# First output tiles multiplied inside the last head pair: an attention layer and its projection in one program

## The reference

```python
z = u_lat @ w_in                                             # 8 x 1024 columns
y_a = z_ab * dwconv(z_ac * z_ax, w_conv) * silu(z_ag)        # short gated convolution
y_b = neighbourhood_attention(q, k, v, k_c, v_c, rpb) * silu(z_bg)   # 16 heads, 8 x 16 window + context
y_lat = concat([y_a, y_b]) @ w_out                           # 2048 x 1024
h_lat = h_lat + gate * y_lat                                 # then RMSNorm and modulation of layer 1
```

## Time and profile before

| | us |
|---|---|
| median of three runs | 2330.8 |
| lowest and highest | 2329.86, 2332.24 |
| profiled execution, its own time | 2330.06 |
| its span | 2328.3 |
| last `weigh` of the attention begins | 1252.63 |
| first product of the projection | 1264.40 |

### The profile page before, as it was taken

One profiled execution on the slowest core, in us unless ns is written; L12 is line 12 of the kernel. 1 busy time (PEld: TensorE's weight loads), 2 busy tenths in 40 slices (PEclk: granted clock), 3 DMA queues, 4 the chain that ended last, 5 costly groups with the idle time before them and its releaser, 6 DMA issues. The chain is left out here.

```text
span 2328.3 us, 33600 instructions
## 1 busy us (share of the span) xinstructions
PE 2248.5 (97%) x11996; PEld 1958.6 (84%) x11996; DVE 1511.3 (65%) x2407; ACT 1167.5 (50%) x1711; POOL 484.9 (21%) x287
## 2 busy tenths in 40 slices
PE   6999999999999999999997999799999999999998
PEld 4788888888888888888885888699999999998787
DVE  4576575765757657577577437648667766776755
ACT  4534544345344453444434324347876777678311
POOL 0232231322313223223230300021122112220000
PEclk9999999999999999999998999899999999999999
DMA  7111221112122112122115656201111111113521
GB/s 292 37 55 52 66 62 65 54 52 66 50 69 63 52 57 58 34 80 64 62 28 205 181 152 180 88 28 55 54 55 55 55 46 64 55 55 127 208 82 63
DMA packets 145223, 187.47 MB, mean 81 GB/s; under 512 B 50360, under 2 KB 108856, under 8 KB 142008
## 3 DMA queue, kind: packets, MB, share of 16 engines
q1 hardware_dynamic: 137592, 166.67, 22.3%
q10 hardware_dynamic: 7488, 18.88, 2.2%
HBM read 155.62 MB, written 29.88 MB: 80 GB/s over the span
## 5 line engine op out<-in xcount | busy, mean ns | idle before, releaser
L956 PE MATMUL ps<-u_hi,w_hi 128*128 128x512 f32 (+1 forms) x1464 | 533.7, 365 | 0.0
L956 PE MATMUL ps<-u_hi,w_lo 128*128 128x512 f32 (+1 forms) x1464 | 519.1, 355 | 0.0
L956 PE MATMUL ps<-u_lo,w_hi 128*128 128x512 f32 (+1 forms) x1464 | 517.8, 354 | 0.0
L956 PEld LDWEIGHTS ps<-u_hi,w_lo 128*128 128x128 f32 x1464 | 276.2, 189 | 40.1
L956 PEld LDWEIGHTS ps<-u_lo,w_hi 128*128 128x128 f32 x1464 | 277.0, 189 | 35.0
L956 PEld LDWEIGHTS ps<-u_hi,w_hi 128*128 128x128 f32 x1464 | 276.5, 189 | 35.1
L2163 PE MATMUL ps<-u_hi,o_w_hi 128*128 128x426 f32 (+2 forms) x640 | 238.2, 372 | 9.4 <-POOL o_w_lo L1738 9.4
L571 ACT ACTIVATE probs<-probs,neg_max 128x640 f32<-128x640 f32 (+1 forms) x160 | 122.8, 768 | 245.4 <-DVE neg_max L772 245.4
L2163 PE MATMUL ps<-u_hi,o_w_lo 128*128 128x426 f32 (+2 forms) x640 | 237.8, 372 | 0.0
L2163 PE MATMUL ps<-u_lo,o_w_hi 128*128 128x426 f32 (+2 forms) x640 | 237.7, 371 | 0.0
L1738 POOL TENSOR_TENSOR o_w_lo<-o_w_raw,o_w_hi 128x1024 fp32r<-128x1024 f32 x48 | 134.5, 2801 | 476.1 <-ACT o_w_hi L1757 476.1
(11 more groups left out here) (221 smaller groups left out, 4601.7 us busy)
## 6 DMA issues: line engine op xcount, KB each, us to landing
w_stage<-in_w_even SPq DMA_DIRECT2D x63, 512.0 KB, 3.5
o_w_raw<-in_w_odd SPq DMA_DIRECT2D x48, 512.0 KB, 3.5
ada_piece<-in_w_ada SPq DMA_DIRECT2D x20, 1024.0 KB, 5.4
y_tile<-y_scratch SPq DMA_DIRECT2D x40, 512.0 KB, 5.2
wout_raw<-in_w_out SPq DMA_DIRECT2D x8, 1024.0 KB, 10.1
y_scratch<-h_backward SPq DMA_DIRECT2D x16, 512.0 KB, 2.6
final_w_raw<-in_w_out SPq DMA_DIRECT2D x8, 1024.0 KB, 10.7
final_y_raw<-y_scratch SPq DMA_DIRECT2D x15, 512.0 KB, 4.3
```

What stands on the lines that cost most here:

```text
L956: last = nc.tensor.matmul(ps[:, bank(j, g), 0:t - f], w[:, slot, c * P:(c + 1) * P], x[:, c, f:t], start=(c == 0 and n == 0), stop=(c == K ...
```

## The change

The blocks `even_layer` and `out_projection(layer=0)` become one. The function `out_projection` is gone; its parts are now in `even_layer`.

- The last pair's 12 conv units all lie in steps 0 to 7 (`LAST_UNITS`). POOL splits the weights of CB and CG two steps earlier (`SPLIT_AFTER_LAST`).
- Steps 8 to 19 of PE multiply the first 56 chunks of pass 0 (`OUT_CHUNKS`: tile, first and last chunk): tiles 0, 1 and 2 and half of tile 3. The rest follows in `projection()`, first tile 3's other half.
- W of pass 0 is loaded over u's latent columns, in two portions as CG's groups 0 and 1 finish with them, and y's even tiles over u's context columns; odd tiles lie over the weights of the layer.
- ACT and DVE split W and y inside the steps: `within(s)` before the units or `copy_low`/`output`, `behind(s)` after them. Two of the gate-row matmuls and the read of tiles 0 and 1 out of their banks lie in the steps too.
- Conv rows are stored in three portions, attention rows of pair 7 in three, so that y's tiles can be loaded earlier.
- W of pass 1 is now loaded once all attention rows are stored, behind the load of y tile 4.
- `odd_layer` has another memory map; its instructions and their order are unchanged.

The diff, cut to its core:

```diff
+LAST_UNITS = ((0,), (1,), (2, 3), (4,), (5, 6), (7,), (8, 9), (10, 11))
...
+OUT_CHUNKS = {8: (0, 0, 5), 9: (0, 5, 11), 10: (0, 11, YC), 11: (1, 0, 5), 12: (1, 5, 11), 13: (1, 11, YC),
+              14: (2, 0, 5), 15: (2, 5, 10), 16: (2, 10, 13), 17: (2, 13, YC), 18: (3, 0, 4), 19: (3, 4, 8)}
+OUT_BEGUN = 4
...
+    SPLIT_AFTER_LAST = {4: CB, 6: CG}
...
-        if not last:
-            return [(j, g, 0, KC) for j, g in (ORDER[s:s + 1] if s < STEPS - 1 else ORDER[s:])]
-        if s < 8:
-            return [(*ORDER[s], 0, KC)]
-        if s < LAT_STEPS:
-            return [(*ORDER[8 + (s - 8) // 2], s % 2 * (KC // 2), (s % 2 + 1) * (KC // 2))]
-        return []
+        if last:
+            return [(*ORDER[u], 0, KC) for u in LAST_UNITS[s]] if s < len(LAST_UNITS) else []
...
+            def projection():
+                i = PAIRS - 1
+                sp.wait_ge(proj, unit(i, CG, 0) + 1)
+                load_out_w(0, 0)
+                load_out_w(0, 1)
+                sp.wait_ge(w_lo, i * 8 + 8)
+                sp.wait_ge(ya_stored, 32 * i + 16)
+                load_y(0, 0, 0)
+                sp.wait_ge(proj, unit(i, CG, 1) + 1)
+                load_out_w(0, 2)
+                load_out_w(0, 3)
+                store_y(i, 0)
+                sp.wait_ge(yb_stored[0], 16 * PAIRS)
+                load_y(0, 0, 1)
+                sp.wait_ge(ya_stored, 32 * i + 48)
+                load_y(1, 1, 0)
+                load_y(1, 1, 1)
+                sp.wait_ge(a_mm, 2 * PAIRS)
+                load_x(0, 0, 0)
+                load_x(0, 1, 1)
+                for t in (2, 3):
+                    for half in range(2):
+                        load_y(t, t, half)
+                load_x(0, 2, 0)
+                store_rest(LAT // 2, LAT, LAT_STEPS)
+                load_x(0, 3, 1)
+                sp.wait_ge(yb_stored[1], 16 * i + 16)
+                for half in range(2):
+                    load_y(4, 4, half)
+                store_rest(LAT, TOK, STEPS)
+                for stored in yb_stored:
+                    sp.wait_ge(stored, 16 * PAIRS + (16 if stored is yb_stored[1] else 0))
+                for q in range(4):
+                    load_out_w(1, q)
+                load_x(0, 4, 0)
+                for t in range(5, NT):
+                    load_tile(0, t, t % 2)
...
+            def out_w_hi(p):
+                act.wait_ge(wo_loaded[p % 8 // 2], 32 * (p // 8 + 1))
+                if p < 8:
+                    nc.scalar.activation(w_pair(uhi, p), w_pair(w0raw, p), ACT.Copy).then_inc(wo_hi, 1)
+                else:
+                    c = slice(2 * p - 16, 2 * p - 14)
+                    nc.scalar.activation(w1hi[:, c, :], w1raw[:, c, :], ACT.Copy).then_inc(wo_hi, 1)
+            def out_y_hi(q, b, half):
+                if isinstance(q, int) and q < 2:
+                    act.wait_ge(proj, unit(PAIRS - 1, CG, NG - 1) + 1)
+                else:
+                    act.wait_ge(mm_done, q + 1)
+                act.wait_ge(y_loaded[half], q * 16 + 16)
+                nc.scalar.activation(y_half(0, b, half), raw_half(half), ACT.Copy).then_inc(y_hi, 1)
+            def copy_gate_row(s):
+                act.wait_ge(row_mm, s + 1)
+                nc.scalar.activation(grow[:, 0, s, :], ps[:, 7, :], ACT.Copy).then_inc(grow_done, 1)
+            def store_half(t):
+                act.wait_ge(h_done, t + 3)
+                act.dma_start(hs[t], h[:, t % 2, :]).then_inc(h_stored[t % 2], 16)
+            def within(s):
+                if s == 7:
+                    out_w_hi(0)
+                    out_w_hi(1)
+                elif s == 8:
+                    out_w_hi(3)
+                    out_y_hi(0, 0, 1)
+                elif s == 9:
+                    out_w_hi(5)
+                elif s == 10:
+                    out_w_hi(7)
+                elif s == 11:
+                    out_y_hi(1, 1, 1)
+                elif s == 13:
+                    out_y_hi(2, 0, 1)
+                elif s == 17:
+                    out_y_hi(3, 1, 1)
+            def behind(s):
+                i = PAIRS - 1
+                if s == 6:
+                    act.wait_ge(ya_done, i + 1)
+                    store_conv(act, i, 0, LAT // 2)
+                elif s == 7:
+                    out_y_hi(0, 0, 0)
+                    out_w_hi(2)
+                elif s == 8:
+                    out_w_hi(4)
+                    act.wait_ge(ya_done, i + 3)
+                    store_conv(act, i, LAT // 2, LAT)
+                    store_conv(act, i, LAT, TOK)
+                elif s == 9:
+                    out_w_hi(6)
+                elif s == 10:
+                    out_y_hi(1, 1, 0)
+                elif s == 12:
+                    copy_gate_row(0)
+                    out_y_hi(2, 0, 0)
+                elif s == 14:
+                    store_half(0)
+                elif s == 16:
+                    copy_gate_row(1)
+                    out_y_hi(3, 1, 0)
+                    store_half(1)
...
+                for t in range(2, NT):
+                    for half in range(2):
+                        out_y_hi(t + 2, t % 2, half)
+                    store_half(t)
+                    if 5 <= t < 9:
+                        out_w_hi(2 * t - 2)
+                        out_w_hi(2 * t - 1)
+                act.wait_ge(row_mm, 3)
+                nc.scalar.activation(grow[:, 1], ps[:, 6:8, :], ACT.Copy).then_inc(grow_done, 1)
...
+            def first_half(t, link):
+                b, s = t % 2, out_stream(t)
+                dve.wait_ge(xh_loaded[b], 16 * (t // 2) + 16)
+                dve.wait_ge(h_stored[b], 16 * (t // 2))
+                dve.wait_ge(grow_done, s + 1)
+                dve.wait_ge(mm_done, t + 3)
+                link(nc.vector.tensor_tensor(h[:, b, :], ps[:, b, :], grow[:, 0, s, :], ALU.mult))
+                nc.vector.tensor_tensor(h[:, b, :], h[:, b, :], xh[:, b, :], ALU.add).then_inc(h_done, 1)
+            half_link = Link(dve, out_links[0])
+            def within(s):
+                if s == 7:
+                    out_w_lo(0)
+                    out_w_lo(1)
+                elif s == 8:
+                    out_w_lo(3)
+                    out_y_lo(0, 0, 1)
+                elif s == 9:
+                    out_w_lo(5)
+                elif s == 10:
+                    out_w_lo(7)
+                elif s == 11:
+                    out_y_lo(1, 1, 1)
+                elif s == 13:
+                    out_y_lo(2, 0, 1)
+                    first_half(0, half_link)
+                elif s == 15:
+                    first_half(1, half_link)
+                elif s == 17:
+                    out_y_lo(3, 1, 1)
+            def behind(s):
+                if s == 7:
+                    out_y_lo(0, 0, 0)
+                    out_w_lo(2)
+                elif s == 8:
+                    out_w_lo(4)
+                elif s == 9:
+                    out_w_lo(6)
+                elif s == 10:
+                    out_y_lo(1, 1, 0)
+                elif s == 11:
+                    dve.wait_ge(ya_stored, 32 * PAIRS + 16)
+                    gate_diagonal(0, 0).then_inc(diag_done, 1)
+                elif s == 12:
+                    out_y_lo(2, 0, 0)
+                elif s == 14:
+                    gate_diagonal(0, 1).then_inc(diag_done, 1)
+                elif s == 16:
+                    out_y_lo(3, 1, 0)
...
+                    if last and s in OUT_CHUNKS:
+                        out_products(*OUT_CHUNKS[s])
...
+                    if last and s == 12:
+                        pe.wait_ge(row_done, PAIRS)
+                        gate_row(0)
+                    if last and s == 16:
+                        pe.wait_ge(mod_copied, PAIRS)
+                        gate_row(1)
                     if s == 14:
+                        if last:
+                            pe.wait_ge(grow_done, 1)
...
+            def out_products(t, c0, c1):
+                if c0 == 0 and t < 2:
+                    last_g = NG - 2 if t == 0 else NG - 1
+                    pe.wait_ge(bank_free[t], half(PAIRS - 1, CG, last_g) + 1)
+                elif c0 == 0:
+                    pe.wait_ge(h_done, t + 1)
+                for c in range(c0, c1):
+                    if c % 8 == 0:
+                        pe.wait_ge(y_lo, 2 * t + (c // 8 + 1))
+                    if t == 0 and c % 2 == 0:
+                        pe.wait_ge(wo_lo, c // 2 + 1)
+                    for n, (y, w) in enumerate(((0, 0), (0, 1), (1, 0))):
+                        ins = nc.tensor.matmul(ps[:, t % 2, :], y_chunk(y, t % 2, c), w_of(0, w, c),
+                                               start=(c == 0 and n == 0), stop=(c == YC - 1 and n == 2))
+                if c1 == YC:
+                    ins.then_inc(mm_done, 1)
...
+            def projection():
+                out_products(OUT_BEGUN - 1, OUT_CHUNKS[STEPS - 1][2], YC)
+                for t in range(OUT_BEGUN, NT):
+                    out_products(t, 0, YC)
```

(49 more changed lines are left out.)

568 lines of the change are left out of this document (226 added, 342 removed).

## The result

| | before | after |
|---|---|---|
| median (4 runs each) | 2330.33 us | 2342.92 us |
| lowest and highest | 2329.19, 2332.24 | 2341.55, 2343.44 |
| span of the profiled execution | 2328.3 | 2339.7 |
| ratio, with its 95% interval | | 1.0054 (1.0042 to 1.0066) |

The kernel became slower by 12.6 us. The direction was forecast; the size was not: 2336 had been said, and the time lies 0.9 us beyond the upper end of the range. The profiled execution grew by 11.4 us, and the rest of this text follows those 11.4 us.

The account below looks back on a forecast made before the run. PE, busy nearly all the time, was taken as the bound. Waits of 17.5 us ended step 19 at 1299.5; 4, 20.9 and 1 more put tile 5 at 1325.4, 5.8 late: 2330.06 + 5.8 = 2336 us, range 2318 to 2342.

Parts of the forecast that it names:

- First half of y tile 0: Step 8's first output product: this half is split by 1224.2, so c=0 begins there instead of 1221.9, costing 2.3 us.
- Second half, held by W's loads: Y tile 0's attention half: its store ends after W, its load lands at 1232, and PE waits 5.2 us.
- Steps 9 and 10: PE waits for ACT's and DVE's splits of W pieces 5 to 7: 2.7 us, then 3.8 us.
- Tile 2 and the context steps: Tile 2 waits for tile 0's bank, 2.7 us; y tile 3's splits delay the maximum in steps 17 and 18, 0.8 us.
- The clock: PE about 45% busy between 1231 and 1250 falls to the lower clock level; 4 us shows, bounds nothing to 7 us.
- POOL's share: A POOL bias mask slows DVE's normalise in step 9 or 10, when DVE is the bound: 1 us.
- W's second half ahead of y tile 5: Pass 1's W loads after the last output's store, with y tile 5 queued behind it: PE waits 4.6 us before tile 5.
- From there PE runs its tiles without a gap.: From output tile 2 of the projection's first pass on, PE was taken to run gapless, so only tile 5's start was compared.
- Every later stage is the same code in both kernels.: Everything behind the projection's early tiles was taken as the same code, so no cost behind tile 5 was counted.
- the splits keep up: Rival, 27%: W's splits in steps 8 to 11 run ahead of PE and the clock stays; 2323 us, down to 2318.
- the stores chain: Rival, 8%: storing y tile 0's conv half during W's first 2 MB takes 8.6 us and delays W's rest; 2342 us.
- the clock stays up: Rival, 20%: PE's stalls are too short to lower the clock; 2331.9 us, no change that can be measured.

Follow-up runs that it names:

- e4: Changed kernel with the last 1 MB piece of the first pass's W loaded behind y tile 0's second half: 2339.97 us, ratio 1.0041.
- e3: Changed kernel with the second pass's four 1 MB W pieces loaded one each behind y tiles 5 to 8: 2333.57 us, ratio 1.0015.
- e12: Changed kernel with only the last layer's map corrected, weights, y tiles and second W at 128 past a multiple of 256: 2337.99 us, ratio 1.0037.
- e6: Changed kernel with pass 1's W pieces spread, last layer's map realigned, and first W's last piece behind y tile 0's second half: 2324.93 us, ratio 0.9982.
- e8: Changed kernel with only the final product's second W moved by 32 bytes: 2342.16 us, ratio 1.0055.
- e2: Kernel before with the last layer's map shifted 32 bytes and a 64-byte pad that moved the first layer's y tiles: 2339.50 us, ratio 1.0046.
- e7: Kernel before with the last layer's map shifted 32 bytes and a 128-byte pad ahead of the first layer's y tiles: 2337.87 us, ratio 1.0040.
- e9: Kernel before with only a 256-byte pad ahead of the first layer's y tiles: 2329.66 us, ratio 1.0001.
- e10: Kernel before with only a 512-byte pad ahead of the first layer's y tiles: 2329.93 us, ratio 0.9998.

## Why the prediction was wrong, step by step

1. **First half of y tile 0** (2.3 us): its chunk c=0 was said to begin at 1224.2 and began at 1224.95. Right. PE's wait was longer, 4.19 us, because PE was ready at 1220.8 and not at 1221.9.
2. **Second half, held by W's loads** (landing 1232, c=8 at 1236.7): ACT split it at 1233.03 and c=8 began at 1237.59. Right. e4 shows the cause: with one W piece behind it, the load that waits for the store's end is issued 3 us sooner after the store. The rule cited from the Trainium skill (DMA: Bandwidth & Descriptors, Queues, rings and completion order) pointed the right way; the runs show the delay and its relief, not the write order inside a DMA engine. PE's wait was 3.6 and not 5.2 us, because the products ahead of it began 0.8 us late and ran for some 3 us at half clock, and so filled a part.
3. **Steps 9 and 10** (2.7 and 3.8): 2.2 and 2.0. Right in kind, large by 2.3.
4. **Tile 2 and the context steps** (2.7 and 0.8): 1.8, and 1.1 + 0.4. Right within 1 us.
5. **The clock** (4 us): from the windows, (0.06 + 0.37 + 0.43) x 4 = 3.4 us of full work lost. Size right, place wrong: two short stretches, behind the waits at 1224.95 and at 1241.40, and none until 1255. The first of them also filled part of item 2's wait, so the two should not have been added in full.
6. **POOL's share** (1 us): the slow normalise came (1.43 us of DVE at 1227.92, while POOL masked a bias piece from 1227.85), but in step 8, ahead of DVE's wait of 3.64 us for the y split: it cost nothing. The last `weigh` ended at 1299.7 where items 1 to 6 make 1304.5: together with PE's start for step 8, 1.1 us too late in the sum, they were 4.8 us too dear.
7. **W's second half ahead of y tile 5** (4.6 us): the wait was 6.4. PE came 16.4 us after the last `weigh` (16.3 was said), and the store was issued 1.5 after it as said; but W's issue to tile 5's product took 19.4 us, the very 19.3 of the earlier trace rows, and I had taken off 2.3 for the loads ahead of y tile 2. That deduction was the mistake: an x half stands ahead of this y tile as well, and it, too, comes after all 4 MB. Tile 5 was thus 2.7 us late, where 5.8 was said.
8. **"From there PE runs its tiles without a gap."** The step that failed first. I priced the wait of item 7 by its length alone, although item 5 had just argued that such waits bring the clock down. The 6.4 us were followed by some 5 us at the lower level, and tile 5 took 13.5 us for 10.9: **2.7 us not in the sum**. e3 takes both away at once and gains 9.4.
9. **"Every later stage is the same code in both kernels."** The step that failed most. The same instructions, but not the same addresses: 5.2 us in the last layer and 0.9 in pass 1, of 11.4. The diff showed the constants moved ahead of `o_w_hi` and I read it as bookkeeping. e12 gives 4.9 of it back with an edit that moves no instruction.

As a sum: 2.7 + 2.7 + 0.9 + 5.2 = 11.5 for the 11.4 of the spans. Up to tile 5 the forecast was 3.1 us too high, and it left out 8.7 behind it.

Of the rivals, "the splits keep up" did not happen (they made PE wait 7.8 us), nor did "the stores chain". That the clock stays up did not happen either. None of them, and no bound of the range, held a cost behind tile 5. The limit of the gain, 21 us, was read rightly as a limit: e6 gets 4.6 of it.

## What to carry to other kernels

When a change alters a memory map, compare the addresses of every matmul's two operands before and after, modulo 256, even in stages whose code it doesn't touch: here 6 of the 11.4 us came of that. Price a wait of the matmul engine together with the clock behind it; and ask of each load queue what the first tile behind a large load needs, since 4 MB in one piece ahead of a tile of 1 MB cost 9 us that four pieces between the tiles did not.

## What the runs showed of the hardware that was not expected

- A 512-column fp32r product follows the one before after 0.2267 us where the stationary and the moving operand start equally far past a multiple of 256 bytes (both at 128, or both at 96 in the changed kernel), and after about 0.2333 where they don't: 0.32 us on a tile of 48. Differences of 32 either way (changed kernel and e8, y at 96 or W at 96) and y 64 ahead of W (e2) cost 0.32 us a tile, 128 (e7) cost 0.28, 256 and 512 (e9, e10) nothing. With W 64 ahead of y (pass 1 of the changed kernel) only 0.09 a tile was lost, where y 64 ahead of W cost 0.29 in the same pass (e2). So the sign matters too; that was not taken apart, and other offsets were not tried.
- Why this is so is not shown. A weight load lasts 0.19 us and overlaps the product ahead of it in the profile, so both operands may be read from SBUF at once. A conflict of the two reads would fit; no run here looks at it. The Trainium skill (SBUF — State Buffer, SBUF: two separate sides) says that PE never waits on anyone on the engines' side. That is about PE beside other engines, which no run here looks at; e8 shows that PE's own pace does depend on where its two operands lie (10.88 or 11.20 us a tile).
- The clock fell and rose again faster than I had reckoned with: after the wait at 1224.95 the products stood 0.43 us apart for some 3 us, then 0.23 again. From 1230 to 1236 the granted clock was 1.00, with PE busy 4.00 of the 6 us.
